# Hybrid attention block on one core: the row of maxima and the repeated reciprocals carried by transfers

## The chip, the cores and the metric

The kernel runs on one core of a Trainium2 chip. The metric is device time in microseconds (us); lower is better. Engines are named as in the profile: PE (TensorE; PEld is its weight load), DVE (VectorE), ACT (ScalarE), POOL (GpSimd) and SP (SyncE), whose instructions start transfers; SPq is SP's queue.

## The reference, cut to what matters

One layer over 2048 rows of 1024 features, in float32. Each of three groups of heads is attended, the outputs are joined, projected by w_o and added to x, and an MLP with squared ReLU follows. The part around the change is this:

```python
s = jnp.einsum('bqhd,bkhd->bhqk', q, k) * scale       # 4 causal heads of width 96, 4 memory heads of width 64
s = jnp.where(mask[None, None], s, NEG)               # causal heads only, by chunks of 64 frames
p = jax.nn.softmax(s, axis=-1)                        # exp(s - max) / sum
o = jnp.einsum('bhqk,bkhd->bqhd', p, v)
...
mixed = jnp.concatenate([out_a, out_b, out_m], axis=-1)
x = x + mixed @ w_o[l]
hf = rms_norm(x, g_ffn[l])
x = x + jnp.square(jax.nn.relu(hf @ w_ff1[l])) @ w_ff2[l]
```

## The kernel before

Three stages follow each other: a front (0 to about 470 us: projections, the sliding-window heads, queries and keys written to memory), `attend_and_project` (about 470 to 1050 us) and the MLP. Nearly all products are made from operands split in a high and a low part, three matmuls for one product (`products`, L126).

**Units, steps, chunks.** `attend_and_project` treats 32 units: for each of four blocks of 512 queries, eight heads, memory heads (two steps) and causal heads (4, 8, 12 or 16 steps) in turn. A step is one tile of 128 keys against the unit's 512 queries: PE makes scores, ACT takes the exponential (`a_prob`), DVE or ACT makes its high part, POOL its low part (L2131), and four steps later PE multiplies by the values. There are 192 steps. The numbers of all work items are put into slots beforehand by a planner (`put(name, slot, item)`); one step is one slot, each engine walks the slots in the same order and waits at semaphores, and the place of an item in its engine's queue is therefore fixed by its slot and by the order of the blocks within a slot.

**The row of maxima.** The maximum of each query must be known before a unit's first step. PE multiplies the high parts in chunks (L2319, two banks `pA` in turn), DVE reduces each chunk (L2247 to L2250) and then negates the maximum over the chunks into `neg_max`, 128 queries on partitions by 4 columns (L2256, `reduced`). Two slots after the last chunk, item `turn`: PE turns the four columns into rows by four transposes into bank `pX` (L2345) and ACT copies the row of 512 into partition 0 of the query tile `q_hi` (L2191, `row_done`). Partition 0 of the key tile holds ones, so that the maximum is subtracted by the product itself. The first step of the unit waits for `row_done`. A causal unit's last chunk lies four slots ahead of its first step where units are long; a memory unit's lies up to 13 ahead. The queries themselves (partitions 1 to D) are loaded by SP (L2041, `q_loaded`).

**The reciprocals.** The values have a column of ones, so that row 64 of a unit's output holds the denominators. ACT copies it into `srow`, partition 32 r for unit r of a group of four units (L2200). After each fourth unit DVE takes reciprocals of `srow` into `rrow` in four instructions (L2273, `inverted`), PE repeats them over 128 partitions by two matmuls per group with the 0/1 matrix `pick` (L2400, float32 operands, two records each in the profile), written into `pX`, and DVE multiplies `mixed` by the bank (L2277, `scaled`). There are 8 groups; the last is done at the end, with its second half in `pO[1]`.

**Bank pX** is shared by three users: `turn`, `spread` and `turn_h` (L2391, the transposes of the normalised rows for the MLP, read by DVE at L2300). Each waits until the other two have been read out (`row_done`, `scaled`, `kept`).

**SP's queue** holds, in each slot and in this order: keys for the chunks (L2036), queries (L2041), low queries (L2046), keys (L2052), values (L2057), w_o (L2061), mixed outputs of the window heads (L2066), rows of x (L2074, L2076), and stores (L2080 to L2092). Loads are placed 7 to 9 slots ahead where their buffer allows it.

Of the kernel before, what the change touches and what calls it, by code (L numbers as in the profile page):

```python
# [7 lines left out]
ALU = mybir.AluOpType  # L8
# [5 lines left out]
P = 128  # L14
# [126 lines left out]
UQ = 512  # L141
# [1598 lines left out]
def attend_and_project(nc, ctx, ident, F, A, S, R, banks, M):  # L1740
# [51 lines left out]
    def put(name, slot, x):  # L1792
        at.setdefault(name, {}).setdefault(slot, []).append(x)
# [15 lines left out]
    for U, x in enumerate(units):  # L1809
        first, last = chunk_slot[x["chunks"][0]], chunk_slot[x["chunks"][-1]]  # L1810
        put("turn", last + 2, U)
        if U >= RQ:
            put("q_load", max(first - 7, end_of(U - RQ)), U)
        if U >= RL:
            put("ql_load", max(x["start"] - 9, end_of(U - RL)), U)
        end = end_of(U) + LAG
        put("stage", end, U)
        if U % 4 == 3:
            last = U + 1 == NUNITS
            for i in range(4):  # L1820
                put("invert", end if last else end + 1 + i, (U // 4, i))
            for i in range(2):
                put("spread", end + 1 if last else end + 6 + i, (U // 4, i))
                put("scale", end + 1 if last else end + 7 + i, (U // 4, i))
        scale_slot.append(end + 1 if U + 1 == NUNITS else end + 8)
    for n in range(len(pieces)):
# [122 lines left out]
    p_hi = [sb(f"p_hi{b}", [P, UQ], F32R) for b in range(RP)]  # L1949
    p_lo = [sb(f"p_lo{b}", [P, UQ], F32R) for b in range(RP)]  # L1950
    srow = [sb(f"srow{b}", [P, UQ]) for b in range(2)]
    rrow = [sb(f"rrow{b}", [P, UQ]) for b in range(2)]
    pick = sb("pick", [P, 2, P])
    part_max = sb("part_max", [P, QT, SEQ // CW])
    neg_max = [sb(f"neg_max{b}", [P, QT]) for b in range(4)]
    zeros = sb("zeros", [P, P])
    assert room["at"] <= 80 * KB

# [20 lines left out]
    q_filled, k_filled = R["q_filled"], R["k_filled"]  # L1979
    kp_loaded, k_loaded, v_loaded, q_loaded, ql_loaded = (R[x + "_loaded"] for x in ("kp", "k", "v", "q", "ql"))  # L1980
    scored, max_done = sem("scored"), sem("max_done")
    reduced, neg_done, row_turned, row_done = sem("reduced"), sem("neg_done"), sem("row_turned"), sem("row_done")
    qk_done, exp_done, pv_done = sem("qk_done"), sem("exp_done"), sem("pv_done")
    hi_act, hi_dve, lo_done = sem("hi_act"), sem("hi_dve"), sem("lo_done")
    staged, inverted, spread, scaled = sem("staged"), sem("inverted"), sem("spread"), sem("scaled")
    wo_loaded = [sem(f"wo_loaded{b}") for b in range(RW)]
    w_hi_done, w_lo_done, g_loaded = sem("w_hi_done"), sem("w_lo_done"), sem("g_loaded")
    swa_loaded = [sem(f"swa_loaded{b}") for b in range(2)]
# [8 lines left out]
    def hi_wait(eng, s):  # L1997
        if s >= 0:
            wait(eng, hi_act if on_act[s] else hi_dve, act_before[s + 1] if on_act[s] else s + 1 - act_before[s + 1])

    def m_of(v):
        return 2 if v == EARLY[-1] else v % 2

# [7 lines left out]
            return pY  # L2011
        return [(pA[0], pA[1]), (pY, pS[0]), (pO[0], pS[1]), (pY, pS[0])][v - NV + QT][a]

    def spread_bank(g, i):

        return pO[1][:, :] if i and g == NUNITS // 4 - 1 else pX[:, :, :].rearrange("p a q -> p (a q)")

    def y_free(v, a):

# [3 lines left out]
    def sync(sp):  # L2023
# [7 lines left out]
        for s in slots:  # L2031
# [5 lines left out]
            for U in of("q_load", s):  # L2037
                hd, b = units[U]["hd"], U % RQ
                D, c_ = hd["D"], cols(units[U]["u"])
                sp.wait_ge(qk_done, end_of(U - RQ))  # L2040
                sp.dma_start(q_hi[1:D + 1, b, :].bitcast(F32), S[hd["q"]][0, 0:D, hd["h"], c_]).then_inc(q_loaded[b], 16)  # L2041
            for U in of("ql_load", s):
                hd, b = units[U]["hd"], U % RL
                D, c_ = hd["D"], cols(units[U]["u"])
                sp.wait_ge(qk_done, end_of(U - RL))
                sp.dma_start(q_lo[1:D + 1, b, :].bitcast(F32), S[hd["q"]][1, 0:D, hd["h"], c_]).then_inc(ql_loaded[b], 16)  # L2046
# [6 lines left out]
            for n in of("v_load", s):  # L2053
                U, j, w = pieces[n]
                hd, b, T = units[U]["hd"], n % VR, CW // P
                sp.wait_ge(pv_done, piece_last[n - VR] + 1)
                sp.dma_start(vals[:, b, 0:w // P, :, :].bitcast(F32).rearrange("p t e d -> p (t e d)"),  # L2057
                             S[hd["v"]][:, hd["h"], j * T:j * T + w // P, :, :].rearrange("p t e d -> p (t e d)")).then_inc(v_loaded[b], 16)
            for k in of("wo_load", s):
                wait(sp, w_lo_done, k + 1 - RW)  # L2060
                sp.dma_start(wo_raw[k % RW][:, :], A["w_o"][0, k * P:(k + 1) * P, :]).then_inc(wo_loaded[k % RW], 16)  # L2061
# [103 lines left out]
    def scalar(ac):  # L2165
        ac.preload_act_table(ACT.Exp)
        ac.wait_ge(const_made, 9)
        for s in slots:
            if 0 <= s < N:
# [15 lines left out]
                if on_act[s]:  # L2185
                    wait(ac, pv_done, s + 1 - RP)
                    ac.activation(p_hi[s % RP][:, :], src[:, :], ACT.Exp, scale=scale).then_inc(hi_act, 1)
            for U in of("turn", s):
                ac.wait_ge(row_turned, U + 1)
                ac.wait_ge(q_loaded[U % RQ], 16 * (U // RQ + 1))  # L2190
                ac.activation(q_hi[0:1, U % RQ, :], pX[0:1, :, :].rearrange("a q p -> a (q p)"), ACT.Copy).then_inc(row_done, 1)  # L2191
            for U in of("stage", s):
                wait(ac, pv_done, end_of(U))
                tile, half = units[U]["hd"]["out"]
                u, g, r = units[U]["u"], U // 4, U % 4
                if u >= 2:
                    ac.wait_ge(m_lo_done, visit_of[QT * (u - 1) - 1, 1] + 1)
                ac.activation(mixed[u % 2][half * VD:(half + 1) * VD, tile, :], pO[U % 2][0:VD, :], ACT.Copy)
                wait(ac, inverted, 4 * (g - 1))
                ac.activation(srow[g % 2][32 * r:32 * r + 1, :], pO[U % 2][VD:VD + 1, :], ACT.Copy).then_inc(staged, 1)  # L2200
            for k in of("wo_split", s):
                ac.wait_ge(wo_loaded[k % RW], 16 * (k // RW + 1))
# [36 lines left out]
    def vector(dve):  # L2239
# [12 lines left out]
        def negate(U):  # L2252
            last = units[U]["chunks"][-1]
            dve.wait_ge(max_done, last + 1)
            wait(dve, row_turned, U - 3)
            dve.tensor_reduce(neg_max[U % 4][:, :], part_max[:, :, 0:chunks[last][2] + 1], AX.X, ALU.max, negate=True  # L2256
                              ).then_inc(reduced, 1)

        for s in slots:
# [9 lines left out]
            for g, i in of("invert", s):  # L2269
                part = slice(i * P, (i + 1) * P)  # L2270
                dve.wait_ge(staged, 4 * (g + 1))
                wait(dve, spread, 2 * (g - 1))
                dve.reciprocal(rrow[g % 2][:, part], srow[g % 2][:, part]).then_inc(inverted, 1)  # L2273
            for g, i in of("scale", s):
                part = mixed[g // 2 % 2][:, (2 if i == 0 else 0) + g % 2, :]
                dve.wait_ge(spread, 2 * g + i + 1)
                dve.tensor_tensor(part, part, spread_bank(g, i), ALU.mult).then_inc(scaled, 1)  # L2277
            for k in of("wo_split", s):
                dve.wait_ge(w_hi_done, k + 1)
                dve.tensor_tensor(w_lo[:, k, :], wo_raw[k % RW][:, :], w_hi[:, k, :].bitcast(F32), ALU.subtract).then_inc(w_lo_done, 1)  # L2280
# [28 lines left out]
    def tensor(pe):  # L2309
        pe.wait_ge(q_filled, 1)  # L2310
        pe.wait_ge(k_filled, 1)
        for s in slots:
            for n in of("chunk", s):
                U, q, ch, w = chunks[n]
                D, w, b = units[U]["hd"]["D"], max(w, 256), chunk_piece[n] % KP
                pe.wait_ge(q_loaded[U % RQ], 16 * (U // RQ + 1))
                pe.wait_ge(kp_loaded[b], 16 * (chunk_piece[n] // KP + 1))
                wait(pe, max_done, n - 1)
                pe.matmul(pA[n % 2][:, 0:w], q_hi[0:D + 1, U % RQ, q * P:(q + 1) * P],  # L2319
                          kp_hi[0:D + 1, b, 0:w], start=True, stop=True).then_inc(scored, 1)  # L2320
            if 0 <= s < N:
                U, k, c0, d0 = steps[s]
                D, n = units[U]["hd"]["D"], piece_at(U, k)
                if s == units[U]["start"]:
                    pe.wait_ge(row_done, U + 1)
                    pe.wait_ge(ql_loaded[U % RL], 16 * (U // RL + 1))
                if s == piece_first[n]:
                    pe.wait_ge(k_loaded[n % KR], 32 * (n // KR + 1))
# [5 lines left out]
                if s == 0:  # L2334
# [1 line left out]
                    pe.wait_ge(q_filled, 3)  # L2336
                products(pe, pS[s % RS][:, c0:], [(kh[0:D + 1, keys], kl[0:D + 1, keys], qh[0:D + 1, c0:], ql[0:D + 1, c0:])]
                         ).then_inc(qk_done, 1)
            for U in of("turn", s):
                pe.wait_ge(reduced, U + 1)  # L2340
                wait(pe, row_done, U)
                wait(pe, kept, count_to("turn_h", s - 1))
                wait(pe, scaled, count_to("spread", s - 1))
                for q in range(QT):
                    ins = pe.transpose(pX[0:1, q, :], neg_max[U % 4][:, q:q + 1], ident[:, :])  # L2345
                ins.then_inc(row_turned, 1)
            r = s - LAG
            if 0 <= r < N:
                U, k, c0, d0 = steps[r]
# [35 lines left out]
            for t, e in of("turn_h", s):  # L2385
                pe.wait_ge(normed, t + 1)
                wait(pe, kept, 2 * t + e)
                wait(pe, row_done, count_to("turn", s))
                wait(pe, scaled, count_to("spread", s - 1))
                for k in range(KH):  # L2390
                    ins = pe.transpose(pX[:, k, :], xn[:, (e * KH + k) * P:(e * KH + k + 1) * P], ident[:, :])  # L2391
                ins.then_inc(turned, 1)
            for g, i in of("spread", s):
                pe.wait_ge(inverted, 4 * (g + 1))
                wait(pe, row_done, count_to("turn", s))
                wait(pe, kept, count_to("turn_h", s))
                wait(pe, scaled, 2 * g + (i if g < NUNITS // 4 - 1 else 0))
                if g == 0:
                    pe.wait_ge(const_made, 9)
                pe.matmul(spread_bank(g, i), pick[:, i, :], rrow[g % 2][:, :], start=True, stop=True).then_inc(spread, 1)  # L2400

    def portions_made(eng):

# [126 lines left out]
```

## Time and profile before

| | |
|---|---|
| median of 3 runs | 2280.0 us (2277.43 to 2280.72) |
| span of the profiled execution | 2274.9 us |
| PE busy | 2174.3 us, 96% |
| DVE, ACT, POOL busy | 1447.4, 1016.2, 1078.7 us |

```profile
## 2 busy tenths in 40 slices
PE   8999999679999999888999999999999999999999
PEld 6898999556777776667888877888888888888887
DVE  5787888867665654546876788777653655354453
ACT  6565665456564555454433353333333233223221
POOL 2565566633455465545866656666535830020220
PEclk9999999879999999999999999999999999999999
DMA  6143233477557475566544474444376763243463
```

Each digit is the busy share, in tenths, of a fortieth of the span (56.9 us); PEclk is the clock granted to PE in tenths of full speed, and DMA is the mean busy share of the 16 DMA engines. The attention stage is slices 9 to 18.

### The profile page before, as it was taken

Reading aid. Unit: us, or ns where it says so; the run is one execution under the profiler, and the core shown is the slowest. Engines: PE = TensorE matmul, PEld = TensorE weight load, DVE = VectorE, ACT = ScalarE, POOL = GpSimd, SP = SyncE. Lnnn points to the kernel's source line nnn. Section 1 sums busy time; section 2 is a strip of 40 time slices with the busy share of each in tenths; the row PEclk is TensorE's granted clock in tenths of the full one; section 3 lists DMA queues with packets and bytes.
Section 4 is the critical chain, followed back from the end, with each engine's and each line's share of the span. In section 5 each row is a group of like instructions: output and inputs, shape, how many; then the busy total and the mean of one; then the engine's idle time right before and its main releaser. Section 6 shows DMA issues by size and latency. Waiting matters only on the chain. (4 is left out here: it accounts for less than half of the span.)

```text
span 2274.9 us, 32134 instructions
## 1 busy us (share of the span) xinstructions
PE 2174.3 (96%) x10280; PEld 1786.0 (79%) x10280; DVE 1447.4 (64%) x2052; ACT 1016.2 (45%) x1751; POOL 1078.7 (47%) x892
## 2 busy tenths in 40 slices
PE   8999999679999999888999999999999999999999
PEld 6898999556777776667888877888888888888887
DVE  5787888867665654546876788777653655354453
ACT  6565665456564555454433353333333233223221
POOL 2565566633455465545866656666535830020220
PEclk9999999879999999999999999999999999999999
DMA  6143233477557475566544474444376763243463
GB/s 233 39 113 80 78 93 83 111 205 220 169 158 231 157 230 157 153 222 187 176 152 152 153 259 141 152 151 151 133 276 241 283 234 111 95 146 105 154 213 121
DMA packets 291405, 370.67 MB, mean 163 GB/s; under 512 B 27280, under 2 KB 186192, under 8 KB 289488
## 3 DMA queue, kind: packets, MB, share of 16 engines
q1 hardware_dynamic: 291280, 369.08, 50.6%
q8 instruction: 69, 1.13, 0.2%
q14 instruction: 56, 0.46, 0.1%
HBM read 244.07 MB, written 124.93 MB: 162 GB/s over the span
## 5 line engine op out<-in xcount | busy, mean ns | idle before, releaser
L126 PE MATMUL bank<-f_t_hi,f_w_hi 128*128 128x512 f32 x896 | 350.7, 391 | 6.6 <-issue 4.0
L2131 POOL TENSOR_TENSOR a_p_lo<-a_prob,a_p_hi 128x512 fp32r<-128x512 f32 (+1 forms) x192 | 230.9, 1207 | 252.8 <-DVE a_p_hi L2268 105.3
L126 PE MATMUL bank<-f_t_hi,f_w_lo 128*128 128x512 f32 x896 | 349.9, 391 | 0.0
L126 PE MATMUL bank<-f_t_lo,f_w_hi 128*128 128x512 f32 x896 | 349.9, 391 | 0.0
L126 PE MATMUL bank<-f_w_hi,f_a_hi 128*128 128x512 f32 x896 | 348.5, 389 | 0.0
L126 PE MATMUL bank<-f_w_lo,f_a_hi 128*128 128x512 f32 x896 | 348.5, 389 | 0.0
L126 PE MATMUL bank<-f_w_hi,f_a_lo 128*128 128x512 f32 x896 | 348.5, 389 | 0.0
L126 PEld LDWEIGHTS bank<-f_t_hi,f_w_hi 128*128 128x128 f32 x896 | 169.0, 189 | 44.3 <-issue 8.7
L1594 DVE TENSOR_TENSOR f_a_lo<-f_a_raw,f_a_hi 128x1024 fp32r<-128x1024 f32 x112 | 158.2, 1412 | 69.9 <-ACT f_a_hi L1521 69.5
L126 PEld LDWEIGHTS bank<-f_t_lo,f_w_hi 128*128 128x128 f32 x896 | 169.0, 189 | 35.0
L126 PEld LDWEIGHTS bank<-f_t_hi,f_w_lo 128*128 128x128 f32 x896 | 168.9, 189 | 35.0
L1496 POOL TENSOR_TENSOR f_r<-f_r,f_y 128x512 f32<-128x512 f32 x24 | 42.0, 1786 | 325.3 <-DMA f_r<-s_x 325.3
L126 PEld LDWEIGHTS bank<-f_w_hi,f_a_lo 128*128 128x128 f32 x896 | 168.2, 188 | 34.9
L126 PEld LDWEIGHTS bank<-f_w_hi,f_a_hi 128*128 128x128 f32 x896 | 168.2, 188 | 34.9
L126 PEld LDWEIGHTS bank<-f_w_lo,f_a_hi 128*128 128x128 f32 x896 | 168.2, 188 | 34.9
L1345 DVE TENSOR_TENSOR f_w_lo<-w_raw,f_w_hi 128x512 fp32r<-128x512 f32 x128 | 154.1, 1204 | 62.2 <-ACT f_w_hi L1341 62.2
L1521 ACT ACTIVATE f_a_hi<-f_a_raw 128x1024 fp32r<-128x1024 f32 x112 | 117.5, 1049 | 79.3 <-DMA f_a_raw<-s_aop 79.3
L126 PE MATMUL p_pP<-w_in_hi,p_xT_hi 128*128 128x512 f32 (+2 forms) x384 | 146.6, 382 | 2.2 <-DVE w_in_lo L323 1.9
L126 PE MATMUL bank<-a_p_hi,a_vals 128*66 128x512 f32 (+2 forms) x384 | 145.1, 382 | 1.9 <-POOL a_p_lo L2131 1.7
L1455 POOL TENSOR_TENSOR f_s<-f_a,f_a 128x512 f32<-128x512 f32 x32 | 46.0, 1437 | 209.8 <-DVE f_a L1584 209.8
L126 PE MATMUL p_pP<-w_in_hi,p_xT_lo 128*128 128x512 f32 (+2 forms) x384 | 142.6, 371 | 0.0
L126 PE MATMUL p_pP<-w_in_lo,p_xT_hi 128*128 128x512 f32 (+2 forms) x384 | 142.0, 370 | 0.0
(304 smaller groups left out, 4802.5 us busy)
## 6 DMA issues: line engine op xcount, KB each, us to landing
f_a_raw<-s_aop SPq DMA_DIRECT2D x112, 512.0 KB, 4.3
w_raw<-in_w_ff SPq DMA_DIRECT2D x64, 512.0 KB, 5.3
s_aop<-f_a SPq DMA_DIRECT2D x128, 256.0 KB, 4.4
s_aop<-f_s SPq DMA_DIRECT2D x96, 256.0 KB, 2.4
f_w_raw<-in_w_ff SPq DMA_DIRECT2D x64, 256.0 KB, 5.3
f_t_raw<-s_hop SPq DMA_DIRECT2D x14, 1024.0 KB, 8.9
f_r<-in_w_ff SPq DMA_DIRECT2D x48, 256.0 KB, 6.0
a_vals<-s_v SPq DMA_DIRECT2D x40, 264.0 KB, 4.4
```

The lines of the kernel that those rows point to most:

```text
L126: ins = pe.matmul(out, a, b, start=(first and j == 0), stop=(last and j == n - 1))
L1345: dve.tensor_tensor(w1_lo[j][:, :, :], left(u, j), w1_hi[j][:, :, :].bitcast(F32), ALU.subtract).then_inc(w_lo_done, 1)
L1455: pool.tensor_tensor(s1[b][:, :], a21[b][:, :], a22[b][:, :], ALU.add).then_inc(a_summed, 1)
L1496: pool.tensor_tensor(xs(q, b), xs(q, b), y[:, b, :], ALU.add).then_inc(x_summed, 1)
L1521: ac.activation(a_hi[a][:, :], a_raw[a][:, :], ACT.Copy).then_inc(a_hi_done, 1)
L1594: dve.tensor_tensor(a_lo[a][:, :], a_raw[a][:, :], a_hi[a][:, :].bitcast(F32), ALU.subtract).then_inc(a_lo_done, 1)
L2131: pool.tensor_tensor(p_lo[s % RP][:, c0:], prob[s % R32][:, c0:], p_hi[s % RP][:, c0:].bitcast(F32), ALU.subtract).then_inc(lo_done, 1)
```

## The change

In 32 units the four transposes on PE and the copy on ACT go. SP waits for `reduced` instead and issues four transfers, each from one column of `neg_max` (128 partitions, 4 bytes each) to 128 consecutive elements of partition 0 of `q_hi`. They raise `q_loaded` of that buffer, so that a unit's queries and row count to 80 and not to 16. In SP's slot they stand behind the loads of chunk keys and queries and ahead of all others. The unit's first step waits for all 80; the chunks wait for the first 16. DVE waits for the transfers of four units ago before it writes `neg_max`.

In the first seven groups the matmuls with `pick` go. DVE inverts `srow` in place, and SP issues four transfers per group, each from one partition of `srow` (512 elements, 2 KB) to 64 partitions of `scales[i]`, 128 KB each, in slot end+5, behind the load of values. DVE's two multiplications stay in slots end+7 and end+8, read `scales` from SBUF, and both wait for all four transfers. The last group keeps its matmuls, which now read `srow`. With `turn` and most of `spread` gone, `turn_h` has no other user of `pX` to wait for.

```diff
             for i in range(2):
-                put("spread", end + 1 if last else end + 6 + i, (U // 4, i))
+                put("spread_here" if last else "spread", end + 1 if last else end + 5, (U // 4, i))
                 put("scale", end + 1 if last else end + 7 + i, (U // 4, i))
...
+    def row_wait(eng, U):
+
+        if U >= 0:
+            eng.wait_ge(q_loaded[U % RQ], 80 * (U // RQ) + 80)
...
+            for U in of("turn", s):
+                sp.wait_ge(reduced, U + 1)
+                for q in range(QT):
+                    with nc.allow_non_contiguous_dma(reason="one maximum per query"):
+                        sp.dma_start(q_hi[0:1, U % RQ, q * P:(q + 1) * P].bitcast(F32), neg_max[U % 4][:, q:q + 1].bitcast(F32)).then_inc(q_loaded[U % RQ], 16)
...
+            for g, i in of("spread", s):
+                sp.wait_ge(inverted, 4 * (g + 1))
+                wait(sp, scaled, 2 * (g - 1) + i + 1)
+                for half in range(2):
+                    r = 32 * (2 * half + i)
+                    sp.dma_start(scales[i][half * VD:(half + 1) * VD, :],
+                                 over_heads(srow[g % 2][r:r + 1, :], VD)).then_inc(spread, 16)
...
-            for U in of("turn", s):
-                ac.wait_ge(row_turned, U + 1)
-                ac.wait_ge(q_loaded[U % RQ], 16 * (U // RQ + 1))
-                ac.activation(q_hi[0:1, U % RQ, :], pX[0:1, :, :].rearrange("a q p -> a (q p)"), ACT.Copy).then_inc(row_done, 1)
...
-            wait(dve, row_turned, U - 3)
+            row_wait(dve, U - 4)
...
-                wait(dve, spread, 2 * (g - 1))
-                dve.reciprocal(rrow[g % 2][:, part], srow[g % 2][:, part]).then_inc(inverted, 1)
+                dve.reciprocal(srow[g % 2][:, part], srow[g % 2][:, part]).then_inc(inverted, 1)
...
-                dve.wait_ge(spread, 2 * g + i + 1)
-                dve.tensor_tensor(part, part, spread_bank(g, i), ALU.mult).then_inc(scaled, 1)
+                if g == LAST:
+                    dve.wait_ge(last_spread, i + 1)
+                else:
+                    dve.wait_ge(spread, 64 * (g + 1))
+                dve.tensor_tensor(part, part, spread_bank(i) if g == LAST else scales[i][:, :], ALU.mult).then_inc(scaled, 1)
...
-                    pe.wait_ge(row_done, U + 1)
+                    row_wait(pe, U)
...
-            for U in of("turn", s):
-                pe.wait_ge(reduced, U + 1)
-                wait(pe, row_done, U)
-                wait(pe, kept, count_to("turn_h", s - 1))
-                wait(pe, scaled, count_to("spread", s - 1))
-                for q in range(QT):
-                    ins = pe.transpose(pX[0:1, q, :], neg_max[U % 4][:, q:q + 1], ident[:, :])
-                ins.then_inc(row_turned, 1)
...
-                wait(pe, row_done, count_to("turn", s))
-                wait(pe, scaled, count_to("spread", s - 1))
...
-                pe.matmul(spread_bank(g, i), pick[:, i, :], rrow[g % 2][:, :], start=True, stop=True).then_inc(spread, 1)
+                pe.matmul(spread_bank(i), pick[:, i, :], srow[g % 2][:, :], start=True, stop=True).then_inc(last_spread, 1)
```

## Rows read from the trace of the kernel before

**Rows 1.** The page's head and its section 1: busy time of each engine.
```profile
span 2274.9 us, 32134 instructions
...
PE 2174.3 (96%) x10280; PEld 1786.0 (79%) x10280; DVE 1447.4 (64%) x2052; ACT 1016.2 (45%) x1751; POOL 1078.7 (47%) x892
```
**Rows 2.** Windows: stretch, length, busy per engine, PE clock, DMA share, GB/s.
```profile
470.00:1010.00 540.00, 504.36 (x2334) 375.66 (x2331) 316.27 (x575) 300.35 (x605) 270.57 (x240) 0.97 0.61 187
1010.00:2275.00 1265.00, 1244.16 (x5468) 1026.99 (x5468) 769.16 (x842) 446.41 (x646) 552.58 (x368) 0.99 0.51 174
```
**Rows 3.** Waits of 470 to 1030 us: waiter, releaser, total, times, longest.
```profile
PE bank L2319 <- DVE a_part_max L2250: 7.0, 5, 2.9
```
**Rows 4.** PE's instructions grouped by line and form: busy, mean ns, idle before.
```profile
L2345 PE MATMUL bank<-ident,a_neg_max 128*1 128x128 f32 x128 | 20.6, 285 | 6.9 <-DVE a_neg_max L2256 4.0 <-DVE a_mixed L2277 3.0
...
L2400 PE MATMUL bank<-a_rrow,a_pick 128*128 128x512 f32 x32 | 16.8, 613 | 6.3 <-DVE a_hT L2300 4.0 <-DVE a_mixed L2277 2.1
```
**Rows 5.** Timeline of PE about a turn and a spread: start, length, instruction.
```profile
713.89 0.40 PE L126 MATMUL bank<-a_q_hi,a_k_lo 97*128 97x512 f32 x1
714.13 0.60 PE L2345 MATMUL bank<-ident,a_neg_max 128*1 128x128 f32 x4
714.48 0.48 PE L126 MATMUL bank<-a_p_hi,a_vals 128*66 128x512 f32 x1
...
843.79 0.39 PE L126 MATMUL bank<-a_w_hi,a_m_lo 128*128 128x512 f32 x1
844.02 1.02 PE L2400 MATMUL bank<-a_rrow,a_pick 128*128 128x512 f32 x2
844.47 0.80 PE L2319 MATMUL bank<-a_kp_hi,a_q_hi 97*128 97x512 f32 x1
```
**Rows 6.** Timeline of PE at two late turns, in brackets the idle time before.
```profile
543.15 0.60 PE L2345 MATMUL bank<-ident,a_neg_max 128*1 128x128 f32 x4 [1.84 <-DVE a_mixed L2277]
...
956.44 0.60 PE L2345 MATMUL bank<-ident,a_neg_max 128*1 128x128 f32 x4 [1.55 <-DVE a_neg_max L2256]
```
**Rows 7.** Windows behind the first of these, columns as in rows 2.
```profile
545.00:549.00 4.00, 4.00 (x15) 3.13 (x14) 1.98 (x4) 2.75 (x4) 1.29 (x1) 0.65 0.53 184
```
**Rows 8.** Timelines of SP, DVE and PE at units 0, 29 and 31.
```profile
469.83 0.44 SPq L2036 DMA_DIRECT2D a_kp_hi<-s_k_mla  x1
...
473.20 0.65 PE L126 MATMUL bank<-a_q_hi,a_k_hi 65*128 65x512 f32 x1
...
903.24 0.43 SPq L2036 DMA_DIRECT2D a_kp_hi<-s_k_mla  x1
...
904.09 0.17 DVE L2256 TENSOR_REDUCE a_neg_max<-a_part_max 128x4 f32<-128x16 f32 x1
...
909.79 0.48 PE L126 MATMUL bank<-a_q_hi,a_k_hi 97*128 97x512 f32 x1
...
963.12 0.40 PE L126 MATMUL bank<-a_q_hi,a_k_hi 97*128 97x512 f32 x1
```
**Rows 9.** Transfers by tensors: KB each, median us from issue to landing.
```profile
a_q_hi<-s_q_mla SPq DMA_DIRECT2D x16, 192.0 KB, 4.2
...
s_q_mem<-p_m_hi SPq DMA_DIRECT2D x16, 128.0 KB, 2.9
...
p_g_qk<-in_swa_k_norm SPq DMA_DIRECT2D x1, 64.0 KB, 21.5
...
p_g_up<-in_mla_kv_a_norm SPq DMA_DIRECT2D x1, 0.5 KB, 8.7
...
a_g_col<-in_g_ffn SPq DMA_DIRECT2D x1, 4.0 KB, 2.4
```
**Rows 10.** Timelines of DVE and SP at the fourth group's reciprocals and first scaling.
```profile
678.22 0.94 DVE L2273 RECIPROCAL a_rrow<-a_srow 128x128 f32<-128x128 f32 x1
...
684.74 0.58 SPq L2057 DMA_DIRECT2D a_vals<-s_v_mem  x1
...
690.39 0.69 DVE L2277 TENSOR_TENSOR a_mixed<-a_mixed,bank 128x512 f32<-128x512 f32 x1
```

More of the change, by code:

```diff
@@ L1951, in attend_and_project @@
     srow = [sb(f"srow{b}", [P, UQ]) for b in range(2)]
-    rrow = [sb(f"rrow{b}", [P, UQ]) for b in range(2)]
+    scales = [sb(f"scales{i}", [P, UQ]) for i in range(2)]
     pick = sb("pick", [P, 2, P])
     part_max = sb("part_max", [P, QT, SEQ // CW])
-    neg_max = [sb(f"neg_max{b}", [P, QT]) for b in range(4)]
+    neg_max = [sb(f"neg_max{b}", [P, QT], F32R) for b in range(4)]
     zeros = sb("zeros", [P, P])
@@ L1981, in attend_and_project @@
     scored, max_done = sem("scored"), sem("max_done")
-    reduced, neg_done, row_turned, row_done = sem("reduced"), sem("neg_done"), sem("row_turned"), sem("row_done")
+    reduced = sem("reduced")
     qk_done, exp_done, pv_done = sem("qk_done"), sem("exp_done"), sem("pv_done")
     hi_act, hi_dve, lo_done = sem("hi_act"), sem("hi_dve"), sem("lo_done")
-    staged, inverted, spread, scaled = sem("staged"), sem("inverted"), sem("spread"), sem("scaled")
+    staged, inverted, spread, last_spread, scaled = sem("staged"), sem("inverted"), sem("spread"), sem("last_spread"), sem("scaled")
     wo_loaded = [sem(f"wo_loaded{b}") for b in range(RW)]
@@ L2012, in y_bank, with spread_bank @@
         return [(pA[0], pA[1]), (pY, pS[0]), (pO[0], pS[1]), (pY, pS[0])][v - NV + QT][a]
-    def spread_bank(g, i):
-        return pO[1][:, :] if i and g == NUNITS // 4 - 1 else pX[:, :, :].rearrange("p a q -> p (a q)")
+    LAST = NUNITS // 4 - 1
+    def spread_bank(i):
+        return pO[1][:, :] if i else pX[:, :, :].rearrange("p a q -> p (a q)")
     def y_free(v, a):
@@ L2198, in scalar @@
                 ac.activation(mixed[u % 2][half * VD:(half + 1) * VD, tile, :], pO[U % 2][0:VD, :], ACT.Copy)
-                wait(ac, inverted, 4 * (g - 1))
+                wait(ac, spread, 64 * (g - 1))
                 ac.activation(srow[g % 2][32 * r:32 * r + 1, :], pO[U % 2][VD:VD + 1, :], ACT.Copy).then_inc(staged, 1)
@@ L2315, in tensor @@
                 D, w, b = units[U]["hd"]["D"], max(w, 256), chunk_piece[n] % KP
-                pe.wait_ge(q_loaded[U % RQ], 16 * (U // RQ + 1))
+                pe.wait_ge(q_loaded[U % RQ], 80 * (U // RQ) + 16)
                 pe.wait_ge(kp_loaded[b], 16 * (chunk_piece[n] // KP + 1))
@@ L2392, in tensor @@
                 ins.then_inc(turned, 1)
-            for g, i in of("spread", s):
+            for g, i in of("spread_here", s):
                 pe.wait_ge(inverted, 4 * (g + 1))
-                wait(pe, row_done, count_to("turn", s))
                 wait(pe, kept, count_to("turn_h", s))
-                wait(pe, scaled, 2 * g + (i if g < NUNITS // 4 - 1 else 0))
-                if g == 0:
+                if i == 0:
                     pe.wait_ge(const_made, 9)
-                pe.matmul(spread_bank(g, i), pick[:, i, :], rrow[g % 2][:, :], start=True, stop=True).then_inc(spread, 1)
+                pe.matmul(spread_bank(i), pick[:, i, :], srow[g % 2][:, :], start=True, stop=True).then_inc(last_spread, 1)
     def portions_made(eng):
```

## The prediction

> **What bounds the kernel now.** I read the page's busy shares first: PE is busy 2174.3 of 2274.9 us, the next engine 64% [rows 1]. PE is the bound as a whole, so removed PE time is worth its full length as long as no other engine takes over. The windows come next, since the change touches one stage: from 470 to 1010 us PE is busy 504.4 of 540 us, DVE 316, ACT 300, POOL 271, and behind it 1244 of 1265 [rows 2]. The MLP is untouched and only shifts. 192 steps in 540 us make 2.8 us a step. The waits of this stage show PE seldom waiting: the largest entry that isn't about bank pX is 7.0 us for DVE's chunk maxima [rows 3]. The grouping by line gives the two groups that the change removes [rows 4]. I don't use their busy times: records of matmuls overlap. I take instead the distance of starts on PE's timeline.
>
> **What goes, on PE.** A turn: the product before starts at 713.89, the one behind at 714.48, 0.59 us apart; a product of 512 columns takes 0.23 us to the next start, so four transposes cost 0.36 [rows 5]. I read the same distance at all 32 turns (first at 469.4, last at 956.4 us). 32 x 0.36 = 11.5 us for the columns themselves; with the idle time ahead of them the 32 distances sum to 20.7 us. A spread: 843.79 to 844.47 is 0.68, less 0.23 is 0.45 [rows 5]; fourteen of them go, 6.3 us, and with their idle time 16.1 us. The idle time is real: PE waits for pX to be read or for the negated maximum, 6.9 us ahead of the turns' matmuls and 6.3 us ahead of the spreads' [rows 4], the rest ahead of their weight loads. Together 36.8 us. One more item hangs on a removed wait: behind the 1.84 us wait at 543.15 [rows 6] the granted clock was 0.65 over 545 to 549 us, with PE always busy [rows 7]. The level below full speed is 1.2 GHz of 2.4; 4 us at 0.65 lose 1.4, about 1.7 us for the whole dip. That gives 38.5 us.
>
> **What goes elsewhere.** ACT loses 32 copies of a row. They hide beside PE, and ACT is 56% busy in the stage [rows 2]: worth nothing. DVE keeps its reciprocals and multiplications. The waits of turn_h for pX also go; they are nearly nil.
>
> **What comes: the rows.** Per unit SP waits for the negated maximum and issues four transfers; PE's first step waits for the last of them. An issue takes 0.43 us [rows 8], so the last starts some 1.5 us after SP is free. Its landing the trace doesn't show: no transfer here goes from a column of SBUF to one partition. Nearest below is g_col, 1024 single elements in 2.4 us; nearest above in the same stage is a load of queries at 4.2 us, with other loads ahead of it; a column of gains of 0.5 KB in the crowded opening took 8.7 us [rows 9]. I take the middle of 2.4 and 4.2, so 4.8 us in all (3.9 to 5.7), since the row is small but queues behind the loads of its slot. Against it stands the distance from the moment that SP could issue (maximum ready, and SP done with what stands before) to the unit's first step. I mapped SP's 390 transfers of the stage onto the planner's slots. Unit 0: SP is done at 470.3, the step is at 473.2 [rows 8], 2.9 us. Unit 29: SP at 903.7, maximum at 904.3, step at 909.8, 5.5 us [rows 8]. Unit 31: 956.4 to 963.1, 6.7 us [rows 6, 8]. Less what the turn itself took, which no longer delays the step, the shortest are 1.9 (unit 0), 3.4 (29), 3.8 (27), 4.6 (31), 5.1 (25), 5.5 (3), 6.3 (1), 6.3 (17), 6.6 (21), 7.0 (13), 7.7 (19), 8.1 (11), 8.2 (2) and 9.2 (23). With 4.8 us PE waits 2.9 + 1.4 + 1.0 + 0.2 = 5.5 us (2.6 to 9.9 for 3.9 to 5.7). One such wait may bring a clock dip of 1.7 us: 7 us. A rule of the Trainium skill speaks against this part (DMA: Bandwidth & Descriptors, Rules for kernel authors): a transfer with a strided last dimension becomes one descriptor per element, and a transpose should not be made by a rearranged plain transfer. Here that is 512 four-byte elements a unit; g_col's 1024 in 2.4 us [rows 9] show no large price, though its writes go to 128 partitions and not to one.
>
> **What comes: the repeats.** SP waits for the reciprocals and issues four transfers of 128 KB; DVE's scaling waits for all. Counted from the moment that SP can issue, the fourth is issued after 1.8 us. Its landing is bounded from below by the store of 128 KB from SBUF, 2.9 us, from above by 21.5 us of the repeated gain in the opening, the row of the same kind (a short source repeated over partitions), but behind megabytes of loads [rows 9]. So 4.7 to 23.3 us. I take 9 us, twice the low end: the source is one partition, unlike that of the store. The gap before the scaling is 6.6, 5.4, 7.2, 5.1, 8.4, 6.1 and 10.3 us for the seven groups; in the fourth SP is free at 685.3 and the scaling starts at 690.4 [rows 10]. DVE then waits up to 3.9 us. Behind it on DVE's queue stand the chunk maxima, the additions into x and the casts; PE has two banks of chunks, so about one step (2.8 us) passes before it stands still. The excess over that is 0.8 + 1.1 + 0.1 = 2 us; since PE arrives sooner than before, 4 us. The Trainium skill has a harsher price (SBUF — State Buffer, Door 1: The DMA port swizzle): all partitions of a small range share one port of some 27 GB/s. As an estimate from that page, 128 KB at 27.2 GB/s is 4.8 us a transfer, 19 us for four in a row; the sum would then be that of the first rival. No row here has a one-partition source.
>
> **What SP's queue pays.** 128 + 28 issues, about 70 us more on a queue now issuing for 198 of 540 us, plus waits of up to 3.4 us for the maximum and up to 6 us for reciprocals. Behind these stand keys, values and rows of x, mostly placed 5 to 9 steps ahead (14 us or more), which covers it. The stage's DMA share is 0.61 [rows 2]; 16 thousand small elements add to it. Between 0 and 5 us; I take 2. Last, a PE that runs 4% faster meets DVE's maxima more often (7.0 us now [rows 3]): 5 us of the gain return as waits (0 to 12).
>
> **Sum.** 38.5 - 7 - 4 - 2 - 5 = 20.5 us. The profiled span becomes 2254.4; the median of the runs lies 5.1 us above the span (2280.0 against 2274.9, launch and spread between runs), hence 2259.5; I say 2259.
>
> **The rivals.** (1) *The repeats come late.* All 64 copies read one partition, and each engine queue serves them before anything behind. Each microsecond beyond 9.8 (mean gap 7.0 plus a step) costs PE seven. Without the 4 us above the gain is 24.5; it is used up at 9.8 + 24.5/7 = 13.3 us, and at 23.3 us the loss is 94 us, time 2350. Halfway, 18 us, it is 57 us, time 2313. For it: the row at 21.5 us and the single source partition. Against: loads of 192 KB within this stage land in 4.2 us [rows 9]. The Trainium skill's page on SBUF, named above, stands for this rival. (2) *The rows come late.* If a row needs as long as the 8.7 us column, 10.2 with the issues, the gaps above (and those up to 10.1) give 59 us of waits instead of 5.5, and 38.5 - 59 - 1.7 - 4 - 2 - 5 is 33 us slower than before, 2313. It decides from 7.8 us on, where the waits reach 27.5. Against: g_col. (3) *The wait only moves.* DVE's maxima and additions take PE's time back; the time stays within 0.2% of 2280. Against: DVE is 59% busy in the stage and itself waits for PE. (4) *All lands early*: rows at 3.9 us, repeats hidden, nothing returned: 38.5 - 2.6 = 36 us, 2244.
>
> **How the numbers follow.** The forecast with its own range 2248 to 2272 has 0.5; rival 1 0.24, rival 2 0.08, rival 3 0.13, rival 4 0.05. What a measurement of this kernel can tell from no change is 0.2%, 4.6 us. Faster 0.55, same 0.13, slower 0.32. The range must reach into both rivals of the other side: 2246 to 2325 leaves out under 0.2. The point is that of the likeliest case.
>
> **What would show it.** Right: no L2345 and one group of L2400; first steps of units 0, 27 and 29 waiting 1 to 3 us for the rows and the others not; DVE's scaling waiting under 4 us for transfers; PE busy about 485 us in a stage some 20 us shorter. Wrong: landings of the repeats above 10 us with chunk products idle behind them (rival 1); most causal units waiting at their first step (rival 2); idle time ahead of L2319 up by 20 us with transfers on time (rival 3).

## The result

The changed kernel takes 2340.6 us (median of 4 runs, 2338.88 to 2342.47), the kernel before 2278.7 us on the same chip: 1.027 times as long, 95% interval 1.0258 to 1.0282. That is 62 us slower; 2259 us was forecast, with a range from 2246 to 2325.

The page of the changed kernel, its head and sections 1 and 2:

```profile
span 2337.1 us, 31800 instructions
## 1 busy us (share of the span) xinstructions
PE 2170.1 (93%) x10124; PEld 1786.9 (76%) x10124; DVE 1440.2 (62%) x2052; ACT 999.8 (43%) x1719; POOL 1081.9 (46%) x892
...
PE   8999999577877898977999999999999999999999
...
PEclk9999999778898999999999999999999999999999
```

Against [rows 1] PE is busy hardly less, and the span is 62.2 us longer. The slices say where: the attention stage, with fives to eights where nines stood, and the clock with them. The stage now has to be cut at points of equal work. I end it at 1060 us in the kernel before and at 1060 plus the difference of the spans in every other one; the MLP behind it is the same. Windows, columns as in [rows 2], first the kernel before, then the changed one:

```profile
470.00:1060.00 590.00, 543.66 (x2503) 407.22 (x2501) 351.73 (x613) 329.34 (x637) 292.50 (x262) 0.97 0.61 190
```
```profile
470.00:1122.20 652.20, 534.72 (x2333) 403.40 (x2334) 347.86 (x615) 313.26 (x605) 292.57 (x260) 0.90 0.69 179
```

PE idles 46.3 us before and 117.5 us after. It is busy 9 us less, less than the columns taken away, since the same matmuls ran at a mean granted clock of 0.90. So the loss is new idle time, 71 us, with a slower clock behind it. The waits of the changed kernel from 460 to 1100 us name the idle time (waiter, releaser, us in total, times, longest):

```profile
DVE a_mixed L2294 <- DMA a_scales<-a_srow: 66.0, 7, 11.9
PE bank L126 <- DMA a_q_hi<-a_neg_max: 36.3, 8, 10.2
PE bank L126 <- DVE a_x L2307: 28.2, 13, 12.2
PE bank L2336 <- DVE a_part_max L2265: 27.5, 9, 9.7
PE bank L2398 <- DVE a_hT L2317: 9.6, 4, 5.1
```

DVE waits for the repeats at all seven groups, 9.4 us each on average. PE's waits for DVE are mostly the same waits passed on: in the kernel before, those for chunk maxima were 7.0 us [rows 3], and those for additions into x were

```profile
PE bank L126 <- DVE a_x L2290: 6.7, 9, 1.4
```

PE's waits for rows, the second line of the list above, are 36.3 us. One place shows repeats and rows together, the second group, on the timelines of SP, DVE and PE, and below them two windows of the same place, columns as in [rows 2]:

```profile
588.50 7.42 SPq L2076 DMA_DIRECT2D a_scales<-a_srow  x4
595.96 6.52 SPq L2053 DMA_DIRECT2D a_q_hi<-a_neg_max  x4
602.52 0.59 SPq L2064 DMA_DIRECT2D a_k_hi<-s_k_mla  x1
...
602.70 0.69 DVE L2294 TENSOR_TENSOR a_mixed<-a_mixed,a_scales 128x512 f32<-128x512 f32 x1 [9.59 <-DMA a_scales<-a_srow]
...
603.94 0.80 PE L126 MATMUL bank<-a_q_hi,a_k_hi 97*128 97x512 f32 x1 [9.77 <-DMA a_q_hi<-a_neg_max]
```

```profile
598.00:602.00 4.00, 0.00 (x0) 0.00 (x0) 0.00 (x0) 0.00 (x0) 0.00 (x0) 0.50 0.73 34
...
606.00:610.00 4.00, 4.00 (x13) 3.21 (x12) 0.95 (x2) 2.42 (x5) 2.09 (x2) 0.50 0.83 295
```

Eight issues that need 0.5 to 0.6 us each elsewhere hold SP for 14 us. The first two repeats are issued in 0.5 and 0.6 us, the fourth takes 4.2 us and the first row transfer behind it 2.8: SP's issues are held while the transfers ahead drain. Between 598 and 602 us no engine computes, while the DMA engines show a share of 0.73 at 34 GB/s, against 187 GB/s at 0.61 in the stage before [rows 2]: they are busy with very little data. Then PE restarts with the clock at 0.50, its lower level, and still has it at 606 to 610.

From the first issue of a group's repeats to DVE's scaling I read 13.7, 14.2, 14.5, 13.4, 14.6, 14.7 and 13.9 us, 14.1 on average. I had taken 9, between bounds of 4.7 and 23.3.

### The profile page after: what moved, and what is told of

Same layout as the page of the kernel before. It is cut to its first block and busy times, and to the rows that moved or that the text cites. A ratio compares the mean times of both kernels' runs of the same rounds, so it can differ in the third digit from the quotient of the medians.

```text
span 2337.1 us, 31800 instructions
## 1 busy us (share of the span) xinstructions
PE 2170.1 (93%) x10124; PEld 1786.9 (76%) x10124; DVE 1440.2 (62%) x2052; ACT 999.8 (43%) x1719; POOL 1081.9 (46%) x892
## 5 line engine op out<-in xcount | busy, mean ns | idle before, releaser
L2203 ACT ACTIVATE a_prob<-bank 128x512 f32<-128x512 f32 x128 | 76.5, 598 | 219.3 <-PE bank L126 216.3
```

What stands on the lines that cost most here:

```text
L2203: ac.activation(dst[:, :], src[:, :], ACT.Exp, scale=scale).then_inc(exp_done, 1)
```

## The experiments

Rows, repeats and the lateness of the scalings were separated. PE's busy and idle time in the stage is read below from windows cut as above.

**Rows alone.** The changed kernel with the repeats of the kernel before:

```diff
-                put("spread_here" if last else "spread", end + 1 if last else end + 5, (U // 4, i))
+                put("spread_here", end + 1 if last else end + 6 + i, (U // 4, i))
...
-                dve.reciprocal(srow[g % 2][:, part], srow[g % 2][:, part]).then_inc(inverted, 1)
+                wait(dve, last_spread, 2 * (g - 1))
+                dve.reciprocal(rrow[g % 2][:, part], srow[g % 2][:, part]).then_inc(inverted, 1)
```

> Only the rows go by transfers; the reciprocals are repeated by matmuls in all groups, as before. Theory A (the repeats are the cost, the rows cost little): the turns' 20.7 us go, and the waits for rows that had no repeats ahead of them in the changed kernel (7.3 at unit 0, 1.8, 2.9, 2.5, 1.5 us) stay, 16 us, with a dip of the clock behind the first: 2274 to 2284 us. Theory B (the rows are the main cost): PE idles 30 us or more for rows, above 2305 us.

Measured: 2277.6 us against 2277.6, ratio 1.0001 (0.9991 to 1.0011). Theory A holds. The rows neither win nor lose. PE's timeline has six waits for rows, 15.1 us; four of them:

```profile
481.73 0.79 PE L126 MATMUL bank<-a_q_hi,a_k_hi 65*128 65x512 f32 x1 [7.35 <-DMA a_q_hi<-a_neg_max]
...
741.98 0.50 PE L126 MATMUL bank<-a_q_hi,a_k_hi 97*128 97x512 f32 x1 [2.85 <-DMA a_q_hi<-a_neg_max]
823.41 0.50 PE L126 MATMUL bank<-a_q_hi,a_k_hi 97*128 97x512 f32 x1 [2.58 <-DMA a_q_hi<-a_neg_max]
869.11 0.50 PE L126 MATMUL bank<-a_q_hi,a_k_hi 97*128 97x512 f32 x1 [0.62 <-DMA a_q_hi<-a_neg_max]
```

These are units 0, 21, 25 and 27; unit 9 (0.98) and unit 31 (0.72) are the others.

**Repeats alone.** The changed kernel with PE's transposes and ACT's copy of the kernel before (the `turn` items back on PE and ACT, those on SP out).

> Only the repeats go by transfers in seven groups; the row of maxima is turned by PE and copied by ACT, as before. Theory A: 16 us of spreads go, DVE waits some 9 us in each of seven groups, nearly all of it reaches PE, and the clock dips behind each wait: 2325 to 2340 us. Theory B: below 2300 us. If both parts add up, the two differences from the kernel before sum to about 62 us; if the rows' waits of 10 us at units 11 and 15 come from repeats ahead of them in SP's queue, the sum is 20 us short of that, unless DVE's wait takes their place.

Measured: 2318.1 us against 2277.6, ratio 1.0177 (1.0158 to 1.0195), 40.5 us slower. The cause is as theory A has it, but the time is 7 us below its lower end. DVE waits 56.9 us at the seven groups, and PE idles 87.1 us of 632.7, 41 us more than in the kernel before. The two parts alone sum to 40.5 us, both together cost 61.9: 21 us belong to neither. PE's waits for rows differ by as much: 36.3 us in the changed kernel against 15.1 with rows alone. In the changed kernel units 11 and 15 wait 9.8 and 10.2 us for their rows, 20 us, with repeats just ahead in SP's queue. Here DVE's wait takes the place of only part of that.

**Is it the single source partition?** The changed kernel, but each transfer reads 64 partitions once, so the factors are not the right ones:

```diff
-                                 over_heads(srow[g % 2][r:r + 1, :], VD)).then_inc(spread, 16)
+                                 srow[g % 2][half * VD:(half + 1) * VD, :]).then_inc(spread, 16)
```

> The changed kernel, but each of the 28 transfers of 128 KB reads 64 partitions of srow once instead of one partition 64 times, so that the scaling factors are not the right ones. Size, count, destination and place in the queue are the same. If the single source partition sets the time: the time from first issue to scaling falls from 14 us (13.4 to 14.7) to 5 to 7 us, SP's issues no longer take up to 4.5 us, time 2255 to 2280 us. If size, count or the state of the queue set it: 14 us and 2340 us as in the changed kernel.

Measured: 2274.5 us against 2277.6, ratio 0.9981 (0.9968 to 0.9994). 66 us of time hang on which partitions are read. From first issue to scaling it takes 4.2 to 8.2 us, 5.9 on average (5 to 7 was expected), so the partitions read set the time, as expected, and not size, count or the state of the queue. The tile `a_scales` in this run (issue durations in ns min/median/max) and in the changed kernel:

```profile
L2076 SPq DMA_DIRECT2D a_scales<-a_srow x28: 497/596/603, 544.9 to 940.2; - x28
...
  DMA a_scales<-a_srow: 8.1, 4
...
DMA to landing us min/median/max: 2.2/2.5/6.0
```
```profile
L2076 SPq DMA_DIRECT2D a_scales<-a_srow x28: 516/597/4482, 542.5 to 996.5; - x28
...
  DMA a_scales<-a_srow: 66.0, 7
...
DMA to landing us min/median/max: 6.3/8.8/11.8
```

Same size, same count: a landing of 2.5 us becomes 8.8, and an issue of 0.6 us up to 4.5.

**Which partitions?** All four transfers read partition 0 or 32 in place of 0, 64, 32, 96, so two of the factors are not the right ones:

```diff
-                    r = 32 * (2 * half + i)
+                    r = 32 * half
```

> The changed kernel, but the four transfers of a group read partitions 0, 64 or 0, 32 in another choice: all four read only partitions 0 and 32 of srow, so two of the factors are not the right ones; size, count and destinations stay. If the limit is a port that partitions 0 and 32 share while 64 and 96 have another (as the Trainium skill has it), the four queue up fully: first issue to scaling 19 to 22 us in place of 14, time 2370 to 2400 us. If the limit is a single partition or the transfer itself: 14 us, 2340 us.

Measured: 2382.2 us in one run, beside 2278.7. The first group takes 21.3 us (540.8 to 562.1 us) where it took 13.7; DVE's seven waits grew from 66.0 to:

```profile
  DMA a_scales<-a_srow: 114.7, 7
DMA to landing us min/median/max: 7.0/12.9/18.3
```

That is 7 us more a group. Since each partition is read twice here, the totals alone could also come from a limit of each single partition. The single landings exclude that. The first and the second transfer of the second group, one from partition 0 and one from partition 32:

```profile
L2076 SPq DMA_DIRECT2D a_scales<-a_srow x1: 542/542/542, 590.6 to 590.6; - x1
DMA to landing us min/median/max: 7.0/7.0/7.0
...
L2076 SPq DMA_DIRECT2D a_scales<-a_srow x1: 596/596/596, 591.2 to 591.2; - x1
DMA to landing us min/median/max: 11.2/11.2/11.2
```

Issued 0.6 us apart, they land 4.8 us apart, and so do the third and the fourth: partition 32 waits for partition 0. In the same group of the changed kernel, with partitions 0, 64, 32 and 96, the landings are 2.5, 2.1 and 3.0 us apart. So 0 and 32 share a limit, and 64 and 96 are not under it. 128 KB in 4.8 us is 27 GB/s; over the whole group, with the 7 us to the first landing, 512 KB in 21.3 us is 25 GB/s, in 14.1 us 37. The Trainium skill (SBUF — State Buffer, Door 1: The DMA port swizzle) puts 0 to 3 and 32 to 35 on one port and 64 to 67 and 96 to 99 on another, some 27 GB/s each; this case agrees with the rate and with 0 and 32 sharing a port apart from the other two; that 64 and 96 share one is not tested by itself.

**Scalings later.** The changed kernel with DVE's part five slots on, some 14 us:

```diff
-                put("scale", end + 1 if last else end + 7 + i, (U // 4, i))
-        scale_slot.append(end + 1 if U + 1 == NUNITS else end + 8)
+                put("scale", end + 1 if last else end + 12 + i, (U // 4, i))
+        scale_slot.append(end + 1 if U + 1 == NUNITS else end + 13)
```

> The changed kernel with DVE's scalings five slots (about 14 us) later; the transfers as they are. If only DVE's wait costs: no wait for the repeats is left and the time is 2255 to 2265 us. If the repeats also hold up what stands behind them in SP's queue: units 11 and 15 still wait 8 to 10 us each for their rows with clock dips behind, 2280 to 2295 us.

Measured: 2321.6 us against 2277.6, ratio 1.020 (1.0176 to 1.0224). Both expected times missed: DVE's wait is gone from the list, and the time is 27 us above the higher one. The second expectation was right that units 11 and 15 still wait, 9.8 and 10.2 us, but the wait has also moved:

```profile
PE bank L126 <- DMA a_q_hi<-a_neg_max: 67.3, 10, 13.6
```

With DVE on time, PE comes sooner to units whose rows stand behind repeats, and now units 9 and 19 wait 13.1 and 13.6 us too, which DVE's stop had hidden.

**Scalings later, rows on PE.** Repeats alone, with the same edit of the slots.

> Repeats by transfers in seven groups, DVE's scalings five slots later, the row of maxima turned by PE and copied by ACT as before. With the rows off SP's queue nothing urgent stands behind the repeats. Theory A (a repeat's price is only who waits behind it, DVE or the rows): no wait for repeats is left, the spreads' 16 us are won against the kernel before: 2258 to 2268 us. Rival (the repeats fill the transfer queues, and keys and values come late too): PE waits for loads in the seven places, 2275 us or more.

Measured: 2262.1 us against 2278.7, ratio 0.9928 (0.9912 to 0.9945). Theory A: with nobody urgent behind it, the same slow transfer costs little. Its landings are as slow as ever (median 9.0 us). The rival has a true part; keys come late, 7.5 us in two places, above all at unit 19:

```profile
697.77 0.77 PE L126 MATMUL bank<-a_q_hi,a_k_hi 97*128 97x512 f32 x1 [6.80 <-DMA a_k_lo<-s_k_mla]
```

**And the rows of memory units by transfer.** The run before, with `turn` on SP for units where

```diff
+    def by_sp(U):
+        return U > 0 and not units[U]["hd"]["causal"]
```

> As the run before, and the rows of the 15 memory units from unit 2 on go by SP's transfers, as in the changed kernel; unit 0 and the 16 causal units keep PE and ACT. Memory units have 8 to 13 slots from their maximum to their first step, causal ones 4 to 6. Theory A: none of these rows is waited for, and 15 turns of 0.36 us and 1.3 us of idle time go: 5 to 8 us less than the run before, 2250 to 2262 us. Rival: rows behind repeats are late even so, or the waits only move to DVE: as the run before or slower.

Measured: 2260.9 us against 2278.7, ratio 0.9921 (0.9905 to 0.9938). PE waits 0.9 us for rows in all. Its runs overlap with those of the run before, so the further gain of 5 to 8 us did not appear. Late keys cost 10.2 us here against 7.5, which is only a part of what is missing; the rest stays open.

**The first unit.** The kernel before with the rows of units 1 to 31 by transfers (`by_sp` is `U > 0`), unit 0 still on PE and ACT.

> The kernel before with the rows of units 1 to 31 by SP's transfers and that of unit 0 still by PE and ACT. Rows alone gave 2277.6 us, no change, with 7.4 us of idle time at unit 0 and a clock at its lower level some 11 us longer. Theory A: unit 0 eats a third of the rows' gain: 2264 to 2271 us. Rival (the gain is eaten by waits for rows and for DVE all over the stage, and unit 1 waits in unit 0's place): 2274 to 2280 us.

Measured: 2271.0 us against 2278.7, ratio 0.9967 (0.9956 to 0.9979), at the upper edge of theory A. Unit 0's row by transfers costs 0.34% or some 8 us (the two ratios compared): its four row transfers follow some 2 MB of w_o and x in the queue.

**Both gains together?** Rows of units 1 to 31 on SP, scalings late, one repeat per slot:

```diff
-                put("spread_here" if last else "spread", end + 1 if last else end + 5, (U // 4, i))
...
+                    for half in range(2):
+                        put("spread", end + 5 + 2 * i + half, (U // 4, i, half))
```

> Rows of units 1 to 31 by SP's transfers, repeats by transfers with late scalings, and the four repeats of a group issued one per slot over four slots, so that the queues drain between them and a row or a key behind waits for at most one repeat (4 us) in place of four (13 us). Theory A (the remaining price of the repeats is what stands behind them in one queue): the two gains (16.5 us of the repeats, 7.7 us of the rows) add up but for some 5 to 10 us of waits: 2258 to 2266 us. Rival (any repeat ahead of a causal unit's row costs its whole length): 2270 us or more.

Measured: 2309.5 us against 2280.6, ratio 1.0126 (1.0107 to 1.0146). Theory A is refuted, and the rival's 2270 us or more holds. Repeats over four slots meet more rows: nine waits for rows of 1.8 us or more, the longest 10.1; with one shorter they are 43.5 us in all. Against the run with late scalings and the four repeats together (ratio 1.020) it is some 17 us faster, of which unit 0's row explains some 8. So pacing helped by about 9 us and did not bring the gains together.

**Another queue.** The four repeats together, issued by ACT in its own queue (`ac.dma_start` with the same waits, before `wo_split`); rows and loads stay with SP.

> As the run before but the four repeats of a group stand together again and are issued from ACT's queue, while rows and loads stay on SP's. Theory A1 (what hurts is SP's in-order queue): rows and keys land in time, ACT stands still for up to 10 us at seven places while its issues are held: about 2275 to 2300 us, with PE waiting for exponentials and not for rows. Theory A2 (what hurts is the 16 DMA engines being occupied by reads of one port): rows wait about as long as when the repeats were on SP's queue, near 2320 us.

Measured: 2306.3 us against 2280.6, ratio 1.0116 (1.0098 to 1.0134), a little outside A1. PE's waits for rows are 17.7 us, not 43 or 67. But SP's transfers are not spared. The second group's repeats are issued by ACT from 576.85 us on. SP's queue at that place, and the landing of unit 11's last row transfer, issued at 577.58 (KB, us from issue to landing):

```profile
575.77 4.18 SPq L2063 DMA_DIRECT2D a_q_hi<-a_neg_max  x4
579.99 4.60 SPq L2074 DMA_DIRECT2D a_k_hi<-s_k_mla  x1
...
a_q_hi<-a_neg_max SPq DMA_DIRECT2D x1, 0.5 KB, 11.2
```

SP's issues are held here too, although no repeat stands in its queue. Unit 11's row is complete 13.0 us after its maximum and unit 15's 12.5 us, against 3.9 and 4.0 with rows alone and 16.5 and 18.7 in the changed kernel. So theory A2 is right about the larger part of the rows' lateness at these two units, though its time is not met; the order of one queue is the smaller part. That PE waits less has a second reason: it comes later itself. At unit 11 it is ready 11.2 us after the maximum, in the changed kernel 6.8, so of its 7.9 us less waiting only 3.5 are an earlier row. What is left of the gain goes on ACT, which stands while its issues are held (first two rows; the last is a share of PE's):

```profile
ACT a_prob L2206 <- issue: 28.8, 4, 7.5
ACT a_prob L2202 <- issue: 7.2, 1, 7.2
...
PE bank L126 <- DMA a_q_hi<-a_neg_max: 17.7, 7, 4.3
```

## Why the prediction was wrong, step by step

**The bound.** Right: PE bounds, and idle time of PE is what was paid.

**What goes on PE.** 36.8 us was too little. I took a spread at 0.45 us from the distance to the next start. The start after that is late as well: in [rows 5] L2319 starts at 844.47; two products follow before the next start at 845.35 on the same timeline, 0.88 us for two instead of 0.46. So a spread costs 0.87 us, and the fourteen cost 6 us more than in the sum. Repeats alone with late scalings show it: PE is busy 530.9 us in the stage against 543.7, with idle time of 47.0 against 46.3. This error was on the good side.

**The rows.** The landing was right in the middle, 3.3 us taken and 3.5 median measured in the run with rows alone, but not where it mattered: the last transfers of units 0, 21 and 25 took 8.2, 7.1 and 5.0 us. The waits came to 15.1 us, forecast were 5.5 and at most 9.9. Unit 0 was mis-sized, 7.35 for 2.9, since the loads of w_o and x in front of it drain for microseconds after SP is done issuing them; I had counted the gap from SP's issue. At unit 21 it was the same with other loads: the maximum was ready at 732.4 us, SP's first row went out at 732.8, and the last landed at 741.9. At unit 25 SP was late as well: the maximum was ready at 813.5 us, and SP's first row went out at 816.6 behind a queue of loads and stores. The issues took 0.6 us each and not the 0.43 of a load. Units 27 and 31 waited 0.6 and 0.7 us, and 29 not at all.

**The repeats: the step that failed.** This is the term of 4 us. Rival 1 was the right mechanism, and its price for lateness too small. The value taken, 9 us, should have been 14; even so my formula, seven times the excess over 9.8 us, gives 30 us for 14.1, where the run with repeats alone has 41 us of new idle time and the changed kernel 71. Three terms are wrong in it. The gap before the scaling was 7.0 us in the kernel before, but DVE waited 9.4 of 14.1 us, so it came after 4.7: PE and DVE, relieved, arrive sooner, and SP, held before, issues later, as I read it; no run separates these two. The step of cover between DVE and PE hardly exists: PE stood 8.1 us in the first group, 12.2 in the fourth and 9.4 in the sixth, because additions into x and chunk maxima stand right behind the scaling on DVE. And I did not charge what stands behind the repeats on SP: 2 us were in the sum for the whole queue. I had written that keys, values and x are 14 us ahead, which is so for most; the rows are not, and they are 20 us of the 62.

**What was wrong besides.** The run that reads 64 partitions has its scalings 5.9 us after the first issue, sooner than the 9 us of the forecast, and still takes 2274.5 us and not 2259. PE waits 21.9 us for rows in it, where the sum had 5.5. For DVE's additions and chunk maxima (L2307, L2265, L2263) it waits 29.1 us, against 17.9 in the kernel before, where the sum had 5 us of gain returned. So even repeats quicker than forecast gain some 3 to 4 us there, and not 20.

**The clock.** I allowed one dip of 1.7 us. 17.8 us of columns by my count were removed and PE got only 9 us less busy, so by difference some 9 us went to a slower clock, or 15 with the spreads at their true cost. In each of the seven waits above 5 us behind unit 0 the clock fell to 0.50, and it came back 4 to 11 us after PE resumed.

**The rivals' chances.** I gave rival 1 0.24 against 0.5 for my forecast, on the ground that loads of 192 KB land in 4.2 us [rows 9]. None of them reads one partition. The row of a short source repeated over partitions had landed at 21.5 us.

The Trainium skill's rule on ports (SBUF — State Buffer, Door 1: The DMA port swizzle), put beside the sum, would have given 19 us for four in a row. An estimate from the same section for two ports that overlap fully is 9.6 us (two times 4.8), and the measured 14.1 us lies between.

## What to carry to other kernels

Moving work from a bound engine to transfers paid here when the reader was later than the transfer and nobody urgent stood behind it: here the same repeats cost 40 us with a reader two slots on and won 16 us with a reader seven slots on. Count a transfer's time by the partitions that it reads as well as by its bytes, and charge it also to each later entry of its queue. Another queue is not a way out by itself: with the repeats in ACT's queue, SP's transfers of the same moments were late too. When a wait is taken away and the time stays, look at who waits in its place before blaming the size of the gain.

## What the runs showed of the hardware

A transfer from one SBUF partition to 64 took 6.3 to 11.8 us to land where the same bytes from 64 partitions took 2.2 to 6.0. Four of them took 14.1 us from partitions 0, 64, 32, 96 and 21.3 us (first group) from 0 and 32 alone, where they landed mostly 4.8 us apart (3.5 to 5.1). While they drained, an issue took up to 4.5 us for the third or fourth of them and 2.2 to 3.3 us for each of the next two entries of the queue, where 0.5 to 0.6 us is usual. With the repeats in ACT's queue, a load of keys on SP's was held 4.6 us, and 128 four-byte elements issued on SP landed after 11.2 us. With rows alone, 128 elements of four bytes from 128 partitions into one partition landed in 3.5 us (1.9 to 8.2, the longest behind some 2 MB of loads), so a row of single elements was as quick as I had taken it.
